# Gate tiles ahead of branch tiles in each column block, two of them before the heads' barrier, and gathered rows in a ring of eight

## The chip, the cores and the metric

The kernel runs on one core of a Trainium2 chip. The metric is device time in microseconds (us). The core has five engines that run their own instruction streams and meet by semaphores: TensorE (PE, matrix products), VectorE (DVE), ScalarE (ACT), GpSimd (POOL) and SyncE (SP, which only issues transfers here).

## The reference, cut to what matters

One decoder layer over 1024 tokens of width 1024. A wide projection feeds three branches (dilated attention, a gated recurrence, attention into memory tokens). The branches are widened, gated by sigmoids, summed and projected; then comes a layer norm, and an expert network that picks 16 of 16,384 experts for each of 8 heads of a token:

```python
branches = jnp.stack([a_out, b_out, c_out], axis=2)
gates = jax.nn.sigmoid((gate_logits + b_gate[layer]).reshape(b, s, N_BRANCHES, D_MODEL))
widened = jnp.einsum('bsgw,gwd->bsgd', branches, w_branch[layer])
merged = jnp.sum(gates * widened, axis=2)
mix = jnp.einsum('bsd,de->bse', merged, w_out[layer])
...
act = jax.nn.gelu(jnp.einsum('td,ted->te', xt, u_tab[it]), approximate=False)
return jnp.einsum('te,ted->td', gt * act, v_tab[it])
```

The gate logits are columns of the same wide projection. The dots of a token with its 128 picked rows of `u_tab` are the "gathered rows" below.

## The kernel before, in words

The layer runs in two halves of 512 tokens. Each half has these stages, parted by barriers (`cross`: TensorE, VectorE and ScalarE each drain, raise `stage`, and wait until all three have): the heads (four heads, 14 projection tiles each and the attention and recurrence work), the gated stage, the output projection, the layer norm with its transposes, and the expert queries. After both halves comes a long last stage that builds the experts' table and multiplies it, some 2300 us.

**The gated stage** runs over 8 column blocks `j` of 128 output columns. Each has six weight tiles: for each branch b a gate tile G*b* (`w_in`, 8 contraction steps, so 24 matmuls) and a branch tile B*b* (`w_branch`, 4 steps, 12 matmuls). The order is G0 B0 G1 B1 G2 B2. G*b* goes to bank `ps[0]`, ScalarE turns it into `sgate` (L1589); B*b* goes to `ps[1]`, VectorE multiplies it with `sgate` into `macc` (L2111) and adds (L2114). After three, VectorE splits the sum into `m_hi` and `m_lo`.

**A weight tile's way.** Every product is made of three: high weights times high and low data (L958, L961), then low weights times high data (L967). There are two sets of weight buffers, 0 and 1, which tiles use in turn. For each tile SyncE loads the raw weights (L651) once the buffer's last tile has been split; ScalarE copies them rounded to `w_hi` (L1383) once TensorE has begun the tile before (`w_used`); GpSimd subtracts to give `w_lo` (L848), which also frees the raw buffer. TensorE begins a tile when its `w_hi` is there, and its last third when `w_lo` is.

**Before the gated stage's branch tiles** VectorE splits the three branches' outputs into `o_hi` and `o_lo` (L2093, L2095, six instructions, `o_split` counts them), which it does after the barrier that follows the heads. B*b* waits for its two.

**Gathered rows.** In the second half the 128 rows of `u_tab` for token block 0 are gathered beside the last stages: GpSimd copies four indices (`icole`, L867) and issues an indirect transfer of 512 KB for each row (L870) into `e_ring`, 4 slots; VectorE takes the dot with `h1_up` (L1881), which frees the slot. Eight rows go with each column block, eight with each pair of output tiles, eight with each four query tiles. GpSimd issues them between its `w_lo` instructions, in the order in which the code names them (`u_rows`), and VectorE takes them in that order too (`e_rows`). The block's `h1e`, `pidxe` and `pgatee` are loaded by SyncE after the heads' barrier (`load_e_block`).

Nothing reorders instructions: on each engine they run as written.

## Time and profile before

| | |
|---|---|
| median of 3 runs | 4224.91 us (4221.99 to 4230.96) |
| the profiled execution's own time | 4228.72 us |
| its span | 4226.6 us |
| TensorE busy | 3707.9 us (88%) |
| VectorE busy | 2705.7 us (64%) |
| GpSimd busy | 1550.9 us (37%) |
| ScalarE busy | 1368.2 us (32%) |
| gated stage, first half | 556.9 to 768.8 us of the span |
| gated stage, second half | 1465.2 to 1689.4 us |

The engines overlap, so busy times do not add up to the span. What a stage could gain is read from the idle times of the engine that the others wait for in it, and from what ended them. Times in the rows are us from the span's start. "issue" means that the engine waited for nothing that the profile shows.

### The profile page before, as it was taken

The numbers are of one execution on the slowest core, as the hardware profiler recorded it, in microseconds if no ns is written. First come the engines' busy times: TensorE is split into PE (matmuls) and PEld (weight loads), VectorE is DVE, ScalarE is ACT, GpSimd is POOL, SyncE is SP. The second block draws the span as 40 slices with busy tenths as digits, with TensorE's granted clock in tenths as the row PEclk, the third lists the DMA queues.
The fourth block names the chain that finished last, engine by engine and source line by source line (L and its number), as shares of the span: only waits on it lengthen the run. The fifth ranks groups of instructions, "written<-read, shape, count | busy, mean of one in ns | idle before, by whom it ended". The sixth has DMA issues, their size and how long they took to land.

```text
span 4226.6 us, 46191 instructions
## 1 busy us (share of the span) xinstructions
PE 3707.9 (88%) x14431; PEld 2459.3 (58%) x14431; DVE 2705.7 (64%) x5477; ACT 1368.2 (32%) x2741; POOL 1550.9 (37%) x1317
## 2 busy tenths in 40 slices
PE   7999989899888799687437989799799999999998
PEld 5777867678777677475113445354354545545763
DVE  1444443307776765649899988988886878842550
ACT  1444443223434433126024042141240513314540
POOL 2555534230000176465455344443454444420000
PEclk8999999899999999796869999899899999999999
DMA  7667623355444377688999999999999999973557
GB/s 242 199 203 228 206 70 90 96 184 161 142 137 141 91 239 240 233 299 303 374 337 408 384 375 376 350 404 368 352 400 403 404 403 405 396 302 127 182 197 275
DMA packets 505249, 1133.37 MB, mean 268 GB/s; under 512 B 37932, under 2 KB 250076, under 8 KB 504832
## 3 DMA queue, kind: packets, MB, share of 16 engines
q1 hardware_dynamic: 336512, 570.42, 39.2%
q0 software_dynamic: 147456, 536.94, 33.3%
q10 hardware_dynamic: 21120, 24.12, 1.6%
q8 instruction: 70, 1.15, 0.1%
q14 instruction: 91, 0.75, 0.1%
HBM read 1044.28 MB, written 89.41 MB: 268 GB/s over the span
## 4 chain that ended last, share of the span: by engine, by line
PE 34%; DVE 13%; DMA 5%; issue 3%; ACT 1%; POOL 0%; DVEq 0%; ACTq 0%
PE ps L1277 26%; DVE u_ring L2212 6%; PE ps L1263 4%; DMA u_ring<-in_peer_u,pidx 4%; PE ps L1310 3%; DMA v_ring<-in_peer_v 1%; DVE hot L2204 1%; DVE hot L2205 1%; DVE split_v L2259 1%; ACT split_v L1688 0%; DVE pick_own L1843 0%; DVE pick_own L1848 0%; DVE got_own L1851 0%; PE h_up L1252 0%; DVE inds_own L1794 0%
## 5 line engine op out<-in xcount | busy, mean ns | idle before, releaser
L1277 PE MATMUL ps<-v_ring,table 128*128 128x512 f32 x3584 | 1595.0, 596 | 22.4 <-DMA v_ring<-in_peer_v 21.2
L899 POOL DMA_INDIRECT u_ring<-in_peer_u,pidx x896 | 861.5, 961 | 1005.1 <-DVE coefe L2212 921.2
L2212 DVE CUSTOM_DVE_ANT_0 u_ring<-u_ring,h_up 128x1024 f32<-128x1024 f32 x896 | 1061.3, 1217 | 157.2 <-DMA u_ring<-in_peer_u,pidx 145.7
L1277 PEld LDWEIGHTS ps<-v_ring,table 128*128 128x128 f32 x3584 | 664.4, 191 | 779.3 <-issue 727.3
L848 POOL TENSOR_TENSOR w_lo<-w_raw,w_hi 128x1024 fp32r<-128x1024 f32 x200 | 442.1, 2216 | 881.3 <-ACT w_hi L1383 875.7
L958 PE MATMUL ps<-x_hi,w_hi 128*128 128x512 f32 x1280 | 525.4, 410 | 68.7 <-ACT w_hi L1383 59.6
L961 PE MATMUL ps<-x_lo,w_hi 128*128 128x512 f32 x1280 | 511.8, 400 | 0.0
L1263 PEld LDWEIGHTS ps<-hot,hot 128*128 128x128 f32 x2048 | 281.1, 203 | 186.3 <-issue 104.9
L1656 ACT ACTIVATE table<-ps 128x512 f32<-128x512 f32 (+3 forms) x256 | 228.9, 894 | 426.4 <-PE ps L1263 370.4
L1644 ACT ACTIVATE hot<-hot,by_slot 128x128 f32<-128x128 f32 x1024 | 321.3, 387 | 111.3 <-DVE hot L2204 99.6
L1263 PE MATMUL ps<-hot,hot 128*128 128x128 f32 x2048 | 293.3, 289 | 61.4 <-DVE hot L2205 38.3
L958 PEld LDWEIGHTS ps<-x_hi,w_hi 128*128 128x128 f32 x1280 | 249.4, 195 | 136.8 <-ACT w_hi L1383 43.6
L967 PE MATMUL ps<-x_hi,w_lo 128*128 128x512 f32 x1280 | 316.3, 389 | 0.0
L2204 DVE TENSOR_TENSOR hot<-keys,by_slot 128x512 f32<-128x512 f32 x256 | 177.0, 692 | 178.5 <-PE ps L1263 155.9
L961 PEld LDWEIGHTS ps<-x_lo,w_hi 128*128 128x128 f32 x1280 | 249.1, 195 | 53.0 <-issue 1.9
L967 PEld LDWEIGHTS ps<-x_hi,w_lo 128*128 128x128 f32 x1280 | 240.3, 188 | 50.0
L1881 DVE CUSTOM_DVE_ANT_0 e_ring<-e_ring,h_up 128x1024 f32<-128x1024 f32 x128 | 155.3, 1221 | 167.1 <-DMA e_ring<-in_peer_u,icole 149.7
L856 POOL TENSOR_TENSOR w_hi<-w_raw,zero 128x1024 fp32r<-128x1024 f32 x56 | 111.5, 1991 | 260.9 <-PE ps L958 122.3
L1310 PE MATMUL ps<-split_v,split_c 128*128 128x512 f32 x768 | 186.3, 398 | 2.5 <-DVE split_v L2259 1.0
L1383 ACT ACTIVATE w_hi<-w_raw 128x1024 fp32r<-128x1024 f32 (+1 forms) x144 | 131.9, 916 | 145.6 <-DMA w_raw<-in_w_branch 41.5
L2205 DVE TENSOR_TENSOR hot<-keys,by_slot 128x512 f32<-128x512 f32 x256 | 175.6, 686 | 0.0
L1310 PEld LDWEIGHTS ps<-split_v,split_c 128*128 128x128 f32 x768 | 139.6, 188 | 49.0 <-DVE split_v L2259 19.5
(294 smaller groups left out, 4077.5 us busy)
## 6 DMA issues: line engine op xcount, KB each, us to landing
v_ring<-in_peer_v SPq DMA_DIRECT2D x576, 512.0 KB
w_raw<-in_w_in SPq DMA_DIRECT2D x104, 512.0 KB
wh_d<-w_hi SPq DMA_DIRECT2D x56, 512.0 KB, 2.7
wl_d<-w_lo SPq DMA_DIRECT2D x56, 512.0 KB, 4.2
w_hi<-wh_d SPq DMA_DIRECT2D x56, 512.0 KB, 3.7
w_lo<-wl_d SPq DMA_DIRECT2D x56, 512.0 KB, 3.7
w_raw<-in_w_peer_q SPq DMA_DIRECT2D x32, 512.0 KB
u_ring<-in_peer_u,pidx POOLq DMA_INDIRECT x896
```

The lines of the kernel that those rows point to most:

```text
L848: pool.tensor_tensor(out=w_lo[b][:, 0:k, :], in0=w_raw[b][:, 0:k, :], in1=w_hi[b][:, 0:k, :].bitcast(F32), op=ALU.subtract).then_inc(w_spl ...
L899: pool.indirect_dma_start(out=u_ring[:, slot_of(n, k), :], out_offset=None, in_=u_tab, in_offset=bass.IndirectOffsetOnAxis(ap=pidx[n % 2][ ...
L958: first = pe.matmul(out, w_hi[b][:, k, :], hi[:, k, :], start=(k == 0), stop=False)
L961: pe.matmul(out, w_hi[b][:, k, :], lo[:, k, :], start=False, stop=False)
L967: last = pe.matmul(out, w_lo[b][:, k, :], hi[:, k, :], start=False, stop=(k == k_n - 1))
L1263: last = pe.matmul(build_bank(item)[:, P * m:P * m + P], hot2[sub % 2][:, m, :], hot1[sub % 2][:, m, :], start=True, stop=True)
L1277: last = pe.matmul(ps[2 * (n % 2) + c][:, :], table[:, row_of(n, i1), :], v_ring[:, j % V_TILES, HALF * c:HALF * c + HALF], start=(n == p ...
L1310: last = pe.matmul(ps[2 * (n % 2) + c][:, :], c_of[:, n % 2, a, :], v[:, HALF * c:HALF * c + HALF], start=(n == p and i == 0 and a == 0 an ...
L1644: last = act.activation(hot1[sub % 2][:, m, :], hot1[sub % 2][:, m, :], ACT.Copy, scale=by_slot[:, 2, t0 + m:t0 + m + 1])
L1656: last = act.activation(table[:, r0:r0 + near, t0:t0 + TOK].rearrange("p i t -> p t i"), src[:, :, 0:near], ACT.Copy)
L2204: dve.tensor_tensor(out=hot1[sub % 2][:, :, :], in0=numbers(NTILE * (n % 2)), in1=of(0), op=ALU.is_equal).then_inc(hot_one, 1)
L2212: dve.tensor_tensor_reduce(out=u_ring[:, slot_of(n, k), :], in0=u_ring[:, slot_of(n, k), :], in1=h1_up[:, :, :].rearrange("p c n -> p (c n)"),
```

## The change

Four things are changed, in both halves where not said otherwise.

1. In a column block the three gate tiles come first, then the three branch tiles: G0 G1 G2 B0 B1 B2. Each has a bank of its own (`ps[0]` to `ps[5]`). With two sets of buffers in turn, G0, G2 and B1 use set 0, and G1, B0 and B2 use set 1.
2. TensorE's G0 and G1 of column block 0 stand ahead of the barrier that follows the heads, and so do ScalarE's three high parts for G0, G1 and G2. Column block 0 stands outside ScalarE's loop.
3. In the second half the raw weights of G0 and G1 are loaded before the heads instead of after them. G2's are loaded ahead of the wait for the barrier, the rest behind it and behind `load_e_block`.
4. The gathered rows have eight slots: `e_ring` and four more (`e_more`), which lie over memory that the branches and the heads use. GpSimd waits once for each four rows (not for each row), and besides for `o_split` 12, which is when all of the second half's branch splits are done. In the gated stage two rows each go behind the `w_lo` of G2, B0, B1 and B2, none behind G0's and G1's. Before, one or two went behind each of the six.

The diff, cut to its core:

```diff
 E_ROWS = 4
+E_SLOTS = 2 * E_ROWS
...
+MID_K = [D // P] * 3 + [4] * 3
...
+        e_more = [nc.alloc_sbuf_tensor_at(f"e_more{i}", [P, D], F32, offset=o)
+                  for i, o in enumerate((where["causal"], where["state"], where["state"] + 4 * D, where["bmv"] + 64))]
...
-        MP = Steps(sem("mid_pe"), "G0 B0 G1 B1 G2 B2".split())
+        MP = Steps(sem("mid_pe"), "G0 G1 G2 B0 B1 B2".split())
...
+        def e_row(s):
+            return e_ring[:, s, :] if s < E_ROWS else e_more[s - E_ROWS][:, :]
...
-                b, m = t // 2, T_MID // 2 + NT_MID // 2 * j + t // 2
-                if t % 2 == 0:
+                b, m = t % 3, T_MID // 2 + NT_MID // 2 * j + t // 2
+                if t < 3:
...
                 load_topk()
+                for t in range(2):
+                    mid_weight(LATER, 0, t)
                 with sp.Fori(0, NH) as h:
...
-                for t in range(2):
-                    mid_weight(LATER, 0, t)
+                mid_weight(LATER, 0, 2)
                 sp.wait_ge(tk_out, 32 * NB + 32)
                 sp.wait_ge(stage, 3 * boundary(1, 1))
                 load_e_block()
-                for t in range(2, NT_MID):
+                for t in range(3, NT_MID):
...
-            def u_rows(first, last, group, slot):
+            def u_rows(first, last, turn):
+                slot = E_SLOTS * turn
                 for k in range(first, last):
-                    s, r, g = k % E_ROWS, k // E_ROWS % 2, group + k // E_ROWS
-                    pool.wait_ge(e_dots, E_ROWS * g + s + 1)
+                    s, r, g = k % E_ROWS, k // E_ROWS, 2 * turn + k // E_ROWS
                     if s == 0:
+                        pool.wait_ge(e_dots, E_ROWS * g + E_ROWS)
                         pool.wait_ge(e_blk, 48)
+                        pool.wait_ge(o_split, 12)
...
                     for t in range(NT_MID):
-                        split_lo_only(t % 2, t0 + T_MID // 2 + NT_MID // 2 * j + t // 2, KD if t % 2 == 0 else NH)
-                        if hf == 1:
-                            u_rows(E_MID * t // NT_MID, E_MID * (t + 1) // NT_MID, E_MID // E_ROWS * j, E_MID * j)
+                        split_lo_only(t % 2, t0 + T_MID // 2 + NT_MID // 2 * j + t // 2, MID_K[t])
+                        if hf == 1 and t >= 2:
+                            u_rows(E_SLOTS * (t - 2) // 4, E_SLOTS * (t - 1) // 4, j)
...
+                def gated(j, t):
+                    it = KD * hf + j
+                    b = t % 3
+                    n = (t % 2, t0 + T_MID // 2 + NT_MID // 2 * j + t // 2)
+                    if t < 3:
+                        pe.wait_ge(MA.sem, MA.after(f"s{b}", it - 1))
+                        last = tile(n, x_hi, x_lo, KD, ps[b][:, :])
+                    else:
+                        pe.wait_ge(MV.sem, MV.after(f"g{b}", it - 1))
+                        pe.wait_ge(o_split, 6 * hf + 2 * b + 2)
+                        last = tile(n, o_hi[:, NH * b:NH * b + NH, :], o_lo[:, NH * b:NH * b + NH, :], NH, ps[3 + b][:, :])
+                    last.then_inc(*MP.mark(f"{'GB'[t // 3]}{b}"))
+                pe.wait_ge(V.sem, V.after("vt2", NH * hf + NH - 1))
+                gated(0, 0)
+                pe.wait_ge(AC.sem, AC.after("q2", NH * hf + NH - 1))
+                gated(0, 1)
                 cross(pe, boundary(hf, 1))
...
-                for t in range(NT_MID):
+                for t in range(2, NT_MID):
                     gated(0, t)
-                    if hf == 1 and t == 0:
+                    if hf == 1 and t == 2:
                         pe.wait_ge(e_blk, 48)
...
-                cross(act, boundary(hf, 1))
-                with act.Fori(0, KD) as j:
+                def mid_hi(j, t):
+                    weight_hi(t % 2, t0 + T_MID // 2 + NT_MID // 2 * j + t // 2, MID_K[t])
+                def mid_gates(j):
                     it = KD * hf + j
                     for b in range(3):
-                        n = t0 + T_MID // 2 + NT_MID // 2 * j + b
-                        weight_hi(0, n)
-                        weight_hi(1, n, NH)
                         act.wait_ge(MP.sem, MP.after(f"G{b}", it))
                         act.wait_ge(MV.sem, MV.after(f"g{b}", it - 1))
-                        act.activation(sgate[:, b, :], ps[0][:, :], ACT.Sigmoid,
+                        act.activation(sgate[:, b, :], ps[b][:, :], ACT.Sigmoid,
                                        bias=cols[:, bass.ds(KD * b + j, 1)]).then_inc(*MA.mark(f"s{b}"))
+                        mid_hi(j, 3 + b)
+                for t in range(3):
+                    mid_hi(0, t)
+                cross(act, boundary(hf, 1))
+                mid_gates(0)
+                with act.Fori(1, KD) as j:
+                    for t in range(3):
+                        mid_hi(j, t)
+                    mid_gates(j)
...
-            dve.sem_inc(e_dots, E_ROWS)
+            dve.sem_inc(e_dots, E_SLOTS)
...
-                            e_rows(2 * b, 2 * b + 2, E_MID // E_ROWS * j, E_MID * j)
+                            e_rows(2 * b, 2 * b + 2, j)
...
-                        dve.tensor_tensor(out=macc[:, min(b, 1), :], in0=ps[1][:, :], in1=sgate[:, b, :], op=ALU.mult).then_inc(*MV.mark(f"g{b}"))
+                        dve.tensor_tensor(out=macc[:, min(b, 1), :], in0=ps[3 + b][:, :], in1=sgate[:, b, :], op=ALU.mult).then_inc(*MV.mark(f"g{b}"))
```

Where the instructions stand. First ScalarE at the end of the first half's heads. L1581 and L1405 are the ends and heads of loops, `stage` is the barrier's semaphore. Before:

```order
L1581 UNCONDITIONAL_BRANCH [waits spilled2,spilled1,spilled0,stage]
L1581 ISA
L1380 REGISTER_ALU [waits w_landed0]
L1383 ACT_TABLE_LOAD [waits w_used0]
L1383 ACTIVATE w_hi0_62<-w_raw0_60 128x1024 [waits w_saved0]
L1383 ACTIVATE w_hi1_63<-w_raw1_61 128x512 [waits w_landed1,w_used1,w_saved1]
L1587 ISA
L1588 ISA [waits mid_pe]
L1589 ISA [waits mid_dve]
L1589 ACT_TABLE_LOAD
L1589 ACTIVATE sgate_122<-ps0,cols_54 128x512
```

The same place in the changed kernel, where L1397 is the high part and L1602 the gate:

```order
L1397 ACTIVATE w_hi0_62<-w_raw0_60 128x1024 [waits w_landed0,w_used0,spilled2,spilled0,spilled1,w_saved0]
L1397 ACTIVATE w_hi1_63<-w_raw1_61 128x1024 [waits w_landed1,w_used1,w_saved1]
L1397 ACTIVATE w_hi0_62<-w_raw0_60 128x1024 [waits w_landed0,w_used0,w_saved0]
L1602 ACT_TABLE_LOAD [waits mid_dve,mid_pe]
L1602 ACTIVATE sgate_122<-ps0,cols_54 128x512 [waits stage]
L1397 ACTIVATE w_hi1_63<-w_raw1_61 128x512 [waits w_landed1,w_used1,w_saved1]
L1602 ACTIVATE sgate_122<-ps1,cols_54 128x512 [waits mid_dve,mid_pe]
L1397 ACTIVATE w_hi0_62<-w_raw0_60 128x512 [waits w_landed0,w_used0,w_saved0]
```

The wait for `stage` has moved behind three high parts, and the first high part no longer has a table load ahead of it. In the row of the gate the wait for `mid_pe` (G0 done on TensorE) now comes ahead of the load of the table.

Then ScalarE's loop over the later column blocks. Before, it is the second part of the fence above (L1383 and L1589, each with a table load). In the changed kernel:

```order
L1394 REGISTER_ALU [waits w_landed0]
L1397 ACTIVATE w_hi0_62<-w_raw0_60 128x1024 [waits w_used0,w_saved0]
L1397 ACTIVATE w_hi1_63<-w_raw1_61 128x1024 [waits w_landed1,w_used1,w_saved1]
L1393 ISA
L1394 REGISTER_ALU [waits w_landed0]
L1397 ACTIVATE w_hi0_62<-w_raw0_60 128x1024 [waits w_used0,w_saved0]
L1600 ISA
L1601 ISA [waits mid_pe]
L1602 ISA [waits mid_dve]
L1602 ACTIVATE sgate_122<-ps0,cols_54 128x512
L1397 ACTIVATE w_hi1_63<-w_raw1_61 128x512 [waits w_landed1,w_used1,w_saved1]
```

No table load is left inside the loop: the block ahead of the loop leaves the sigmoid's table in place, and the copies run with it.

Last, GpSimd in the second half's gated stage, from the first `w_lo` that has a gather behind it. Before, this is G0's:

```order
L848 TENSOR_TENSOR w_lo_64<-w_raw_60,w_hi_62 128x1024 [waits w_split0]
L864 ISA
L867 ISA [waits e_blk,e_dots]
L867 COPY icole<-pidxe 128x4
L868 REGISTER_ALU
L870 DMA e_ring<-in_peer_u,icole 128x1024 [waits e_idx]
L848 TENSOR_TENSOR w_lo_65<-w_raw_61,w_hi_63 128x512 [waits w_split1]
L864 REGISTER_ALU
L870 DMA e_ring<-in_peer_u,icole 128x1024 [waits e_dots]
L847 ISA
L848 TENSOR_TENSOR w_lo_64<-w_raw_60,w_hi_62 128x1024 [waits w_split0]
```

In the changed kernel it is G2's (the third of the block), and L856 is `w_lo`, L877 the index copy, L880 the gather:

```order
L856 TENSOR_TENSOR w_lo_64<-w_raw_60,w_hi_62 128x1024 [waits w_split0]
L874 ISA
L877 ISA [waits o_split,e_blk,e_dots]
L877 COPY icole<-pidxe 128x4
L878 REGISTER_ALU
L880 DMA e_ring<-in_peer_u,icole 128x1024 [waits e_idx]
L880 DMA e_ring<-in_peer_u,icole 128x1024
L856 TENSOR_TENSOR w_lo_65<-w_raw_61,w_hi_63 128x512 [waits w_split1]
L880 DMA e_ring<-in_peer_u,icole 128x1024 x2
L855 ISA
L856 TENSOR_TENSOR w_lo_64<-w_raw_60,w_hi_62 128x512 [waits w_split0]
```

The index copy now waits for `o_split` besides, and B0's `w_lo` (128x512, buffer 65) stands behind it and behind two gathers.

## Rows read from the trace of the kernel before

**Rows 1.** Windows view, TensorE's idle span, both gated stages: us, busy us by engine, clock

```profile
544.60:556.90 12.30, 0.01 (x1) 0.01 (x1) 9.28 (x9) 10.01 (x9) 0.05 (x1) 0.61 0.00 0
556.90:768.80 211.90, 202.58 (x864) 162.29 (x864) 72.49 (x58) 74.25 (x86) 95.77 (x48) 0.99 0.31 91
585.30:768.80 183.50, 175.63 (x756) 140.82 (x756) 57.90 (x49) 64.66 (x75) 82.73 (x42) 1.00 0.32 92
1465.20:1689.40 224.20, 208.57 (x868) 166.12 (x868) 136.97 (x195) 74.21 (x86) 162.18 (x128) 0.97 0.71 232
1494.30:1689.40 195.10, 180.09 (x756) 144.00 (x756) 115.11 (x176) 64.61 (x75) 137.78 (x112) 0.97 0.71 235
1523.00:1527.00 4.00, 4.00 (x12) 3.09 (x12) 3.07 (x7) 0.63 (x1) 3.19 (x3) 0.57 0.06 16
```

**Rows 2.** Timeline of TensorE, first half: start, us, instruction, [idle before, releaser]

```profile
556.92 0.77 PE L958 MATMUL ps<-x_hi,w_hi 128*128 128x512 f32 x1 [12.31 <-ACT w_hi L1383]
...
585.32 0.50 PE L958 MATMUL ps<-x_hi,w_hi 128*128 128x512 f32 x1 [0.91 <-ACT w_hi L1383]
...
594.22 0.50 PE L958 MATMUL ps<-x_hi,w_hi 128*128 128x512 f32 x1 [0.45 <-ACT w_hi L1383]
```

**Rows 3.** Timeline of ScalarE, around the first barrier and in the loop

```profile
551.94 0.63 ACT L1418 ACTIVATE msum<-msum 128x512 f32<-128x512 f32 x1
554.42 1.28 ACT L1383 ACT_TABLE_LOAD   x1 [1.85 <-DVEq L574]
555.72 1.06 ACT L1383 ACTIVATE w_hi<-w_raw 128x1024 fp32r<-128x1024 f32 x1
...
582.91 1.28 ACT L1383 ACT_TABLE_LOAD   x1 [0.32 <-DMA w_raw<-in_w_in]
...
591.24 1.28 ACT L1589 ACT_TABLE_LOAD   x1 [4.68 <-PE ps L967]
...
593.12 1.05 ACT L1383 ACTIVATE w_hi<-w_raw 128x1024 fp32r<-128x1024 f32 x1
...
1520.35 1.28 ACT L1383 ACT_TABLE_LOAD   x1 [2.31 <-DMA w_raw<-in_w_in]
```

**Rows 4.** Timeline of SyncE's queue, two raw-weight loads

```profile
578.30 0.37 SPq L651 DMA_DIRECT2D w_raw<-in_w_in  x1
...
1513.90 0.37 SPq L651 DMA_DIRECT2D w_raw<-in_w_in  x1
```

**Rows 5.** Timeline of VectorE, the branch split, and a gathered row

```profile
554.15 1.23 DVE L2093 CAST o_hi<-branch 128x2048 fp32r<-128x2048 f32 x1
555.41 2.29 DVE L2095 TENSOR_TENSOR o_lo<-branch,o_hi 128x2048 fp32r<-128x2048 f32 x1
557.62 3.40 DVE L2093 CAST o_hi<-branch 128x2048 fp32r<-128x2048 f32 x1
...
1519.04 1.22 DVE L1881 CUSTOM_DVE_ANT_0 e_ring<-e_ring,h_up 128x1024 f32<-128x1024 f32 x1 [0.91 <-DMA e_ring<-in_peer_u,icole]
```

**Rows 6.** Timeline of GpSimd, second half's gated stage

```profile
1472.96 1.27 POOL L848 TENSOR_TENSOR w_lo<-w_raw,w_hi 128x512 fp32r<-128x512 f32 x1
...
1509.25 0.18 POOL L867 COPY icole<-pidxe 128x4 uint32 x1
1510.24 0.98 POOL L870 DMA_INDIRECT e_ring<-in_peer_u,icole  x1 [0.81 <-POOL icole L867]
1511.24 2.42 POOL L848 TENSOR_TENSOR w_lo<-w_raw,w_hi 128x1024 fp32r<-128x1024 f32 x1
1513.82 0.95 POOL L870 DMA_INDIRECT e_ring<-in_peer_u,icole  x1 [0.16 <-issue]
```

**Rows 7.** Timeline of TensorE, second half

```profile
1522.76 0.50 PE L958 MATMUL ps<-x_hi,w_hi 128*128 128x512 f32 x1 [2.90 <-ACT w_hi L1383]
...
1697.09 0.79 PE L958 MATMUL ps<-m_hi,w_hi 128*128 128x512 f32 x1 [7.89 <-ACT w_hi L1383]
```

**Rows 8.** Waits of GpSimd, second half's output projection: us, times, longest

```profile
POOL icole L867 <- DVE dotse L1881: 3.8, 2, 3.0
```

More of the change, by code:

```diff
@@ L73 @@
 E_ROWS = 4
+E_SLOTS = 2 * E_ROWS
 E_GROUPS = SLOTS // E_ROWS
[L75 to L77 removed]
+OUT_TURN = D // P
+PQ_TURN = OUT_TURN + D // P // 2
 C_Q, C_K, C_V = 0, G * NH * P, 2 * G * NH * P
@@ L385, in layer @@
         coef = coefe
+        assert where["bmv"] + 64 + 4 * D <= r_head and where["state"] + 8 * D <= where["w_raw0"]
+        e_more = [nc.alloc_sbuf_tensor_at(f"e_more{i}", [P, D], F32, offset=o)
+                  for i, o in enumerate((where["causal"], where["state"], where["state"] + 4 * D, where["bmv"] + 64))]
         split_v = [[nc.alloc_sbuf_tensor_at(f"split_v{part}_{i}", [P, D], F32R, offset=where["u_ring"] + (2 * i + part) * D * 4)
@@ L476, in layer @@
         e_blk = sem("e_blk")
-        e_in = [sem(f"e_in{s}") for s in range(E_ROWS)]
+        e_in = [sem(f"e_in{s}") for s in range(E_SLOTS)]
         e_idx, e_moved = sem("e_idx"), sem("e_moved")
@@ L1871, in topk_gates, with e_rows @@
                                   in1=tk.gsm[:, 1, :].unsqueeze(2).to_broadcast([P, PH, TOPK]), op=ALU.mult).then_inc(*TK.mark("gate"))
-            def e_rows(first, last, group, slot):
+            def e_rows(first, last, turn):
+                slot = E_SLOTS * turn
                 for k in range(first, last):
-                    s, r, g = k % E_ROWS, k // E_ROWS % 2, group + k // E_ROWS
+                    s, r, g = k % E_ROWS, k // E_ROWS, 2 * turn + k // E_ROWS
                     if s == 0:
@@ L1879, in e_rows @@
                         dve.wait_ge(e_moved, g + 1)
[L1880 to L1881 removed]
+                    dve.wait_ge(e_in[k % E_SLOTS], 16 * turn + 16)
+                    dve.tensor_tensor_reduce(out=e_row(k % E_SLOTS), in0=e_row(k % E_SLOTS), in1=h1_up[:, :, :].rearrange("p c n -> p (c n)"), scale=1.0, scalar=0.0,
                                              op0=ALU.mult, op1=ALU.add, accum_out=dotse[:, r, s:s + 1]).then_inc(e_dots, 1)
                     if s == E_ROWS - 1:
[L1884 removed]
+                        dve.wait_ge(e_dots, E_ROWS * g + E_ROWS + E_SLOTS)
                         dve.tensor_copy(coefe[:, bass.ds(slot + k - s, E_ROWS)], dotse[:, r, :]).then_inc(e_moved, 1)
```

31 lines of the change are left out of this document (9 added, 22 removed).

## The prediction

> **What bounds the kernel now.** I read the windows view over the stages first, then TensorE's timeline for its idle times and their releasers, then the timelines of the engines that those name. TensorE is what the others wait for in the gated stages. In a column block of the first half it stands twice for ScalarE's high part: 0.45 us at G1 and 0.6 to 0.9 us at the next G0 [rows 2]; blocks 1 to 7 take 183.5 us, 26.2 each. In the second half the same seven take 195.1 us, 27.9 each [rows 1]: there the raw weights are late. All three gate tiles used buffer set 0, so that each began with a chain of w_lo 2.4, raw load, high part 1.06. A load without gathers beside it takes from 578.30 to 582.9, 4.6 us [rows 3, 4]; with them, from 1513.90 to 1520.35, 6.45 us [rows 3, 4], and TensorE then stood 2.9 us and fell to the lower clock [rows 1, 7].
>
> **Part 1: two tiles ahead of the barrier.** It sounds as if 10.9 us of work went into the 12.3 us gap. It does not, for the high part of G0 still stands on ScalarE behind the last head's tail, which ends at 551.94 + 0.63 = 552.6 [rows 3]. What goes is the wait for the barrier, 1.85 us, and a table load, 1.28 us: the high part starts near 552.8, ends near 553.9, and TensorE starts near 554.1, 2.8 us earlier than at 556.92 [rows 2, 3]. G0 keeps its half clock. G0 and G1 then end near 567. But TensorE is now the last at the barrier, and VectorE's split of the branches, which began at 554.15, begins near 567.4. Its six instructions take 3 x (1.23 + 2.29) = 10.6 us if nothing disturbs them; beside GpSimd's w_lo the same copy took 3.40 us [rows 5]. I take 11.8, so the third split is there at 579.2. G2 ends at 573.1, B0 at 575.8, B1 at 578.5, B2 waits 0.7 and ends near 582.2, and the next G0 follows: 3.1 us ahead of 585.32 [rows 2]. Bounds: 0 (the split at 13.9 as disturbed by two w_lo of 5.3 us, and a drain of about 1 us) to 4.
>
> **Part 2: gates first, own banks, no table loads in the loop.** Each loop turn now lacks two loads of 1.28 us [rows 3]. At G1 the chain of load, gate and high part made the 0.45 us and goes whole. At the next G0 what is late next is the raw load: it is issued when B1's w_lo is done. From the block's start: B0 starts at 16.4, high part of B1 until 17.6, w_lo (1.27, [rows 6]) until 19.0, raw load (4.6 with issue) until 23.6, high part until 24.8, so TensorE starts near 24.9 instead of 24.6, and a stop costs 0.25 more, since the first matmul takes 0.50 instead of 0.39 and the pipe refills [rows 2]. A block takes 25.2 us instead of 26.2: 7.0 us over seven. Bounds: 0.4 a block (load 0.9 us slower) to 1.6 (no stop), so 3 to 11.
>
> The Trainium skill (ScalarE: Activation LUTs, "What ACT_TABLE_LOAD costs") puts a switch at 1283 ns and a drain of some 1380 ns more. The load agrees [rows 3]; here the high part starts 0.02 us behind its load, without a drain. By the page the two loads would have cost 5.3 us a turn and part 2 would bring up to 11 us.
>
> **Part 3: the second half's block 0.** Start near 1462.4, again 2.8 us early, G1's end near 1475.5, barrier, G2 until 1481.3, h1_up until 1482.6, B0's high products until 1484.5. The e block and B0's raw weights are issued behind the barrier and are there by 1482, about in time. The price lies on GpSimd: it waits for `o_split` 12 behind G2's w_lo, and B0's w_lo is queued behind that wait and two gathers. The split ends at 1475.8 + 10.8 = 1486.6. Then index copy and its wait 1.0, two gathers 2.3, w_lo 1.3 [rows 6]: near 1491.4. TensorE stands 7 us there, which brings the lower clock again for 4 us (2 us lost). B2's w_lo and the next G0's raw load are late too, by 2 us and 1 us. I lay the next G0 at 1502.5 against 1494.3 before [rows 1]: 8 us lost. Bounds: 4 to 12. Nothing hides it; VectorE's dots only come later.
>
> **Part 4: blocks 1 to 7 of the second half.** GpSimd's work is the same, three w_lo of 2.42, three of 1.3, two index copies of 1.0 and eight gathers of 1.25 [rows 6], 23.2 us with gaps, but it is laid anew: none of it behind G0 and G1, where it waits for raw weights, all of it behind the rest. Its round is w_lo G0 2.4, raw load of G2 4.6, high part 1.2, w_lo G2 2.4, copy and two gathers 3.3, w_lo B0 1.3, two gathers 2.4, w_lo B1 1.3, copy and two 3.3, w_lo B2 1.3, two 2.4: 25.9 us, above TensorE's 24.6. With gathers beside the loads a load takes up to 1.85 us more and there are two on the round (G2's and the next G0's). I take 26.5 between 25.9 and 29.6, nearer the low end because the gathers in flight are fewest when G2's load runs. Against 27.9 that gives 1.4 x 7 = 9.8 us. Bounds: -12 to +14. The eight slots take away GpSimd's waits for dots, which in this stage were none above the gaps of issue.
>
> **Part 5: the edges behind.** At the stage's end VectorE takes the last two dots, then m_hi and m_lo, then comes the barrier; TensorE idled 7.9 us [rows 7]. The last gather now starts about 0.4 us behind B2's end; landing 5.2 [rows 5, 6], dot 1.3, copy and splits 1.6, barrier to product 1.3: 9.8 us, so 1.9 lost (bounds 0 to 4). In the output projection GpSimd stood 3.8 us in two waits for dots [rows 8]; the ring takes them, but behind the longer one its w_lo would have waited for a high part that was itself late by its raw load. I take 1.5 (0 to 3.8). The query tiles: 0.5 (0 to 2.5). Loading two raw tiles before the second half's heads brings nothing: their high parts did not wait for them.
>
> **The sum**, in the profiled execution's own time: 3.1 + 7.0 - 8.0 + 9.8 - 1.9 + 1.5 + 0.5 = 11.9, some 12 us gained (the 2.8 us of the second half's early start are in its 8.0). The last stage does not change and moves as a whole. Its 4228.7 lies 3.8 us above the median of 4224.9, inside the runs' spread, so I subtract from the median, and since the load under gathers is more likely longer than I took than shorter, I take off 1 us: 4224.9 - 11 = 4214.
>
> **The rivals.**
> - *A (slower): the bunched gathers stretch the raw loads.* In blocks 1 to 7 of the second half both loads on GpSimd's round take the 6.45 us of [rows 3, 4]: 29.6 us a block, 1.7 x 7 = 12 us lost where 9.8 was won. With block 0 at its bound of 12 lost and the edges 3 lost: 3.1 + 7 - 12 - 12 - 3 + 1 = -16, so 4241. It decides from a block of about 28.9 us on, or a load of 6.1 us. For it: eight gathers now fall in 60% of the block. Against: G2's load runs while no gather is issued. Chance 0.12.
> - *B: second half breaks even or worse, the first half carries it all.* Block 0 loses 8, the blocks win 4 to 6, edges lose 1: total near 6, 4219, no change by measurement. Chance 0.28.
> - *C: the ring and the order free GpSimd fully.* Block at 25 us in both halves, block 0 loses 5: 3.1 + 8 - 5 + 18 + 1 = 25, so 4200. Against: the 25.9 us round. Chance 0.12.
> - *D: the tiles ahead of the barrier fill the whole gap.* It would need ScalarE's high part before its tail ends; the order shows it behind. 9 us more in each half; chance 0.02.
> - My forecast: 0.46.
>
> **How the numbers follow.** A measurement here tells about 0.2%, 8.4 us, from no change. Faster is C, D, 0.39 of the forecast's 0.46 (its terms spread by about 5 us) and 0.03 of B: 0.56. Slower is A less its mild cases: 0.10. The same is the rest, 0.34. The range reaches to C's outer half and to A's inner third: 4201 to 4228.
>
> **What would show it.** In the profile after: TensorE's first product of each gated stage 2 to 3 us earlier, not 10; no table loads in the loop, stops at G1 gone; a single wait of TensorE for GpSimd's w_lo of about 7 us in the second half's block 0, with the index copy behind the last `o_lo`; first half's seven blocks at 25.2 us, second half's at 26.5 us; the idle at the stage's end near 9.8 us. I am wrong if the second half's blocks take over 28 us, if the splits don't hold GpSimd, or if B2 of block 0 waits over 3 us in the first half.

## The result, and the profile after

| | before | after |
|---|---|---|
| median | 4224.91 us | 4237.87 us (4233.01 to 4239.97) |
| ratio of the times | 1 | 1.0028, 95% interval 1.0017 to 1.0040 |
| span of the profiled execution | 4226.6 us | 4236.0 us |

The change made the kernel 0.28% slower, some 12 us. The forecast was 11 us faster, 4214, with a range of 4201 to 4228. It was wrong in sign, and the time lies outside the range.

The windows view of the changed kernel, to be laid beside [rows 1]: the idle ahead of the first gated stage, that stage up to its last product, its block 0, its blocks 1 to 7, and in the second half the whole stage, its blocks 1 to 7, and 4 us behind the stop in block 0. The columns are those of [rows 1].

```profile
546.80:555.80 9.00, 0.01 (x1) 0.00 (x0) 6.18 (x7) 8.61 (x8) 0.01 (x1) 0.65 0.00 0
555.90:758.60 202.70, 200.02 (x864) 164.34 (x864) 69.56 (x59) 54.81 (x72) 93.16 (x48) 0.98 0.32 93
555.80:587.00 31.20, 28.47 (x108) 22.71 (x109) 17.39 (x10) 8.20 (x10) 17.11 (x7) 0.88 0.27 77
587.00:758.60 171.60, 171.58 (x757) 141.70 (x755) 52.27 (x50) 46.61 (x62) 76.15 (x41) 1.00 0.33 96
1457.30:1689.20 231.90, 210.18 (x868) 165.33 (x868) 123.84 (x193) 54.76 (x72) 155.15 (x128) 0.97 0.68 220
1496.60:1689.20 192.60, 178.74 (x756) 141.47 (x756) 106.03 (x174) 46.56 (x62) 135.57 (x112) 0.99 0.73 235
1485.70:1489.70 4.00, 3.91 (x9) 3.13 (x10) 2.10 (x3) 0.00 (x0) 3.33 (x5) 0.50 0.92 307
```

The first half does what was hoped and more: 202.7 us instead of 211.9, and in blocks 1 to 7 TensorE is busy for 171.58 of 171.6 us. The second half's stage went from 224.2 to 231.9 us, though its blocks 1 to 7 gained 2.5. So what was lost is in its block 0. Some more was lost outside the two gated stages. TensorE's timeline of the changed kernel, only the rows that began after a wait:

```profile
582.65 0.47 PE L968 MATMUL ps<-o_hi,w_hi 128*128 128x512 f32 x1 [2.40 <-issue]
...
939.38 2.07 PE L1014 MATMUL h_up<-skt_side,qs_side 128*128 128x128 f32 x8 [4.81 <-DMA qs_side<-qp_d]
...
1485.79 2.07 PE L977 MATMUL ps<-o_hi,w_lo 128*128 128x512 f32 x4 [6.13 <-POOL w_lo L856]
...
1496.62 0.50 PE L968 MATMUL ps<-x_hi,w_hi 128*128 128x512 f32 x1 [1.48 <-ACT w_hi L1397]
...
1560.72 0.47 PE L968 MATMUL ps<-x_hi,w_hi 128*128 128x512 f32 x1 [1.80 <-ACT w_hi L1397]
...
1700.50 0.80 PE L968 MATMUL ps<-m_hi,w_hi 128*128 128x512 f32 x1 [11.32 <-ACT w_hi L1397]
...
1723.78 0.79 PE L968 MATMUL ps<-m_hi,w_hi 128*128 128x512 f32 x1 [7.83 <-ACT w_hi L1397]
```

The same places in the kernel before:

```profile
945.88 1.38 PE L1004 MATMUL h_up<-skt_side,qs_side 128*128 128x128 f32 x8 [1.99 <-DVEq L574]
...
1715.54 0.80 PE L958 MATMUL ps<-m_hi,w_hi 128*128 128x512 f32 x1 [4.00 <-issue]
```

Read them as five places. At 939 the first score product of the second half waits for its queries, where it waited 2.0 us for the barrier before. At 1485.79 is the stop that the forecast described. At 1560.72 TensorE stops at G1 of a later block; the next G0s have stops too, as at 1496.62. At 1700.50 the idle behind the gated stage has grown from 7.9 [rows 7] to 11.3 us. At 1723.78 a stop in the output projection has doubled.

By stages, each number the difference of the starts of two such rows in one trace (the two traces of each kernel; the heads and the last stage scatter):

| stage | before, twice | after, twice |
|---|---|---|
| first gated stage to first product of the projection | 216.2, 216.4 | 207.1, 206.4 |
| that to first scores of the second half | 172.8, 173.3 | 176.4, 177.1 |
| scores to second G0 (heads) | 519.3, 517.1 | 517.9, 513.0 |
| second G0 to first product of the projection | 231.9, 228.4 | 243.2, 242.7 |
| output projection to query tiles | 97.7, 97.8 | 99.7, 98.5 |
| query tiles to key_f | 104.6, 106.5 | 103.0, 104.7 |
| last stage | 2327.2, 2329.1 | 2332.7, 2332.0 |

Without the heads and the last stage, which the change does not touch, these stages take 823.2 and 822.4 us before, 829.5 and 829.4 us after: some 7 us lost by the traces.

### The profile page after: what moved, and what is told of

The parts are those of the page before. It is cut to its first block, busy times and chain, and to the rows that moved or that the text cites. A ratio compares the mean times of both kernels' runs of the same rounds, so it can differ in the third digit from the quotient of the medians.

```text
span 4236.0 us, 46052 instructions
## 1 busy us (share of the span) xinstructions
PE 3717.9 (88%) x14431; PEld 2468.9 (58%) x14431; DVE 2689.4 (63%) x5477; ACT 1326.3 (31%) x2711; POOL 1542.2 (36%) x1317
## 3 DMA queue, kind: packets, MB, share of 16 engines
q1 hardware_dynamic: 336512, 570.42, 39.3%
## 4 chain that ended last, share of the span: by engine, by line
PE 33%; DVE 14%; DMA 5%; issue 2%; ACT 1%; POOL 0%; DVEq 0%; ACTq 0%
PE ps L1291 26%; DVE u_ring L2236 6%; DMA u_ring<-in_peer_u,pidx 4%; PE ps L1277 4%; PE ps L1324 2%; DVE split_v L2283 1%; ACT split_v L1711 1%; DMA v_ring<-in_peer_v 1%; DVE hot L2228 1%; DVE hot L2229 1%; PE h_up L1266 0%; DVE pick_own L1866 0%; DVE pick_own L1871 0%; DVE got_own L1874 0%; ACT split_c L1710 0%
## 5 line engine op out<-in xcount | busy, mean ns | idle before, releaser
L856 POOL TENSOR_TENSOR w_lo<-w_raw,w_hi 128x1024 fp32r<-128x1024 f32 (+1 forms) x200 | 443.3, 2218 | 880.2 <-ACT w_hi L1397 874.2
L1397 ACT ACTIVATE w_hi<-w_raw 128x1024 fp32r<-128x1024 f32 (+1 forms) x144 | 132.1, 917 | 396.2 <-PE ps L968 144.6
```

The lines of the kernel that those rows point to most:

```text
L856: pool.tensor_tensor(out=w_lo[b][:, 0:k, :], in0=w_raw[b][:, 0:k, :], in1=w_hi[b][:, 0:k, :].bitcast(F32), op=ALU.subtract).then_inc(w_spl ...
```

## The experiments

Each ratio is against the kernel before, run in turn with it on the same chip. The last column is the sum of the stages above without the heads and the last stage, in the run's trace; the kernel before has 823.2 and 822.4.

| run | ratio | 95% interval | stages, us |
|---|---|---|---|
| the change itself | 1.0028 | 1.0017 to 1.0040 | 829.5, 829.4 |
| x1_raw_back | 1.0002 | 0.9992 to 1.0013 | 834.5 |
| x2_group | 1.0004 | 0.9994 to 1.0014 | 828.9 |
| x3_spread | 0.9975 | 0.9966 to 0.9984 | 821.6 |
| x4_projdots | 1.0010 | 1.0001 to 1.0019 | 829.1 |
| y1_shift | 0.9980 | 0.9968 to 0.9991 | 818.5 |
| y2_ring_alone | 1.0000 | 0.9988 to 1.0011 | 824.0 |
| y3_ring4 | 1.0009 | 1.0000 to 1.0019 | 823.6 |
| y4_small | 0.9969 | 0.9960 to 0.9979 | 815.6 |
| z3_half | 0.9965 | 0.9952 to 0.9978 | 810.4 |
| z4_barrier_back | 0.9997 | 0.9985 to 1.0009 | 820.0 |
| w1_first_half | 0.9971 | 0.9960 to 0.9983 | 818.8 |

The variants ran in four series on four chips, and none of these holds the changed kernel beside them, but for one execution: 4229.68 us, beside 17 of the kernel before with a median of 4227.67. So what a variant gains over the changed kernel by the difference of two ratios is uncertain by some 7 us. In all eleven runs that difference is also larger than what the traces show, by 2 to 16 us. So 1.0028 may lie somewhat above the change's usual cost: the spans of the two pairs of traces differ by 9.4 and 3.3 us. Where times and traces disagree below, the size of a part is taken from the trace.

**x1_raw_back.**

```diff
-                for t in range(2):
-                    mid_weight(LATER, 0, t)
                 with sp.Fori(0, NH) as h:
...
-                mid_weight(LATER, 0, 2)
+                for t in range(3):
+                    mid_weight(LATER, 0, t)
```

> The changed kernel, with the raw weights of the second half's G0 and G1 loaded behind the heads again, as before the change. Theory (a small load behind big ones): in the changed kernel TensorE waited 4.8 us for the first queries at the start of the second half's heads, because two raw loads of 512 KB stood ahead of theirs on SyncE's queue, and only 2.0 us before the change; that wait goes back to about 2, the heads end 4 to 5 us sooner, and G0's high part still finds its weights. About 4233 against 4238. Rival (the wait is the query load's own, whatever stands ahead): no difference, 4238, the 4.8 us stay.

Measured: 1.0002 instead of 1.0028. The wait is gone, and G0's high part was not late (TensorE's idle ahead of it is 9.05 and 9.06 us). TensorE's first scores in this run:

```profile
932.47 1.15 PE L1013 MATMUL h_up<-skt_side,qs_side 128*128 128x128 f32 x8 [2.15 <-DVEq L581]
```

SyncE's queue in the changed kernel and, behind it, before:

```profile
930.67 1.00 SPq L658 DMA_DIRECT2D w_raw<-in_w_in  x2
932.09 2.73 SPq L687 DMA_DIRECT2D qs_side<-qp_d  x1
```

```profile
939.62 0.39 SPq L680 DMA_DIRECT2D qs_side<-qp_d  x1
```

The issue of the queries' load alone took 2.73 us instead of 0.39, behind 1 MB of raw weights which nobody needed for 500 us. In the eight traces with the raw loads ahead of it this issue took 2.06 to 3.56 us, in the other seven 0.39. TensorE stood 2.8 us longer and ran at the lower clock behind it (granted 0.55 from 940 to 946). The trace shows 3 us for the wait and its clock; the time moved by more (0.26%, 11 us, with an uncertainty of about 7). The first theory stands, with 3 us by the trace; the 11 us are not shown. The same code in the later stages was slower in this trace (195.2 us for blocks 1 to 7), so that its sum of stages can't settle the size.

**x2_group.**

```diff
-                        pool.wait_ge(o_split, 12)
+                        if r == 1:
+                            pool.wait_ge(o_split, 12)
```

> The changed kernel, but GpSimd waits for o_split 12 only before the second four of each eight gathers (the new slots, which lie over the branches' memory), not before the first four. Theory (the queue behind the wait): B0's w_lo is no longer behind the splits, the stop of 6.1 us in the second half's block 0 goes; the next wait is at B2, whose w_lo now stands behind the o_split wait and two gathers: 1.5 to 3 us. Gain 3 to 5 us, 4233 to 4235 against 4238. Rival (the splits set it): GpSimd's w_lo and index copy now run beside VectorE's splits, which take 13 us instead of 10.5, so TensorE waits for o_split instead and gains 0 to 1 us: 4237.

Measured: 1.0004. Block 0 took 37.0 us instead of 39.3, so 2.3 of the 6 to 8 us that the stop cost. VectorE's splits were not slower (10.5 us in both), which refutes the rival. It was GpSimd that was, once the e block had landed and its index copy could go at 1473.11. Its timeline:

```profile
1474.25 2.45 POOL L881 DMA_INDIRECT e_ring<-in_peer_u,icole  x1 [0.96 <-POOL icole L878]
1477.01 2.71 POOL L881 DMA_INDIRECT e_ring<-in_peer_u,icole  x1 [0.30 <-issue]
1479.74 1.27 POOL L856 TENSOR_TENSOR w_lo<-w_raw,w_hi 128x512 fp32r<-128x512 f32 x1
```

A gather's instruction took 2.45 and 2.71 us beside the splits, where it takes 0.95 elsewhere [rows 6]. So B0's w_lo still came 3.2 us late. Neither theory had that, though the trace of the kernel before has it too, with 2.59 and 2.83 us. In the six traces where gathers run beside VectorE's splits, all twelve of them took 2.45 to 2.83 us; none of the 1966 others took over 1.46.

**x3_spread.**

```diff
+                for t in range(NT_MID):
+                    split_lo_only(...)
+                    if hf == 1 and t >= 2:
+                        u_rows(E_SLOTS * (t - 2) // 4, E_SLOTS * (t - 1) // 4, 0)
-                with pool.Fori(0, KD) as j:
+                with pool.Fori(1, KD) as j:
...
-                        if hf == 1 and t >= 2:
-                            u_rows(E_SLOTS * (t - 2) // 4, E_SLOTS * (t - 1) // 4, j)
+                        if hf == 1:
+                            u_rows(E_SLOTS * t // NT_MID, E_SLOTS * (t + 1) // NT_MID, j)
```

> The changed kernel, with the gathers of column blocks 1 to 7 of the second half laid behind all six w_lo (1, 1, 2, 1, 1, 2), as before the change, instead of 0, 0, 2, 2, 2, 2. Theory (bunching makes G1's raw load late): in the changed kernel these blocks took 27.5 us, with stops of 0.2 to 1.9 us at G1 because B2's w_lo ends late and G1's raw weights are loaded behind it. Spread, the stop at G1 goes and a new one may come at G2: 26.5 us a block, 7 us less, 4231. Rival (the number of gathers counts, not their place): GpSimd's round is the same, and the gathers now run beside G0's and G1's raw loads as well, 27.5 to 28 a block: 4238 to 4241.

Measured: 0.9975, as the theory had it. Its blocks 1 to 7 in the windows view:

```profile
1493.50:1679.80 186.30, 177.36 (x756) 144.91 (x756) 111.15 (x176) 46.62 (x62) 136.27 (x113) 0.97 0.77 249
```

That is 26.6 us a block against 27.5. The number of gathers and GpSimd's busy time are the same (136 us), only their place differs. It also leaves less idle behind the stage, 8.9 us instead of 11.3.

**y4_small.** The gathers of this stage have 64 bytes a row; the rest of each row is left out, and the dots read these bytes again and again.

```diff
-                    pool.indirect_dma_start(out=e_row(k % E_SLOTS), out_offset=None, in_=u_tab,
+                    pool.indirect_dma_start(out=e_row(k % E_SLOTS)[:, 0:w], out_offset=None, in_=u_tab if w == D else u_small,
```

> The changed kernel, with the gathers of the second half's gated stage fetching 16 elements of a row (64 bytes) instead of 1024; the dots read these 16 again and again, over 1008 elements. So part of the gathered data is left out, while GpSimd's and VectorE's instructions stay. Theory (contention): the raw loads come back to 4.6 us, GpSimd's round is 25.9 us, and blocks 1 to 7 take 25.9 to 26.3 instead of 27.5: 9 to 11 us less, 4228. Rival (GpSimd's own time is the bound, not the memory): the blocks stay at 27 or more: 4235 to 4238.

Measured: 0.9969, more than expected. Its blocks 1 to 7:

```profile
1495.60:1674.30 178.70, 175.71 (x757) 140.57 (x756) 109.52 (x175) 46.68 (x63) 134.69 (x113) 1.00 0.34 95
```

25.5 us a block, with the same busy time of GpSimd. This separates the two: 2.0 us a block, 14 us in all (12 against the second trace), is what the gathers' traffic costs through the raw loads. G1's raw weights show it best, whose load starts as the gathers behind B1 and B2 are in flight. The issue on SyncE's queue (the first of a row that holds two) and the high part that waits for it, changed kernel:

```profile
1551.38 5.20 SPq L658 DMA_DIRECT2D w_raw<-in_w_in  x2
```

```profile
1559.52 1.06 ACT L1397 ACTIVATE w_hi<-w_raw 128x1024 fp32r<-128x1024 f32 x1 [6.39 <-DMA w_raw<-in_w_in]
```

With small gathers:

```profile
1547.05 5.23 SPq L659 DMA_DIRECT2D w_raw<-in_w_in  x2
```

```profile
1550.93 1.06 ACT L1398 ACTIVATE w_hi<-w_raw 128x1024 fp32r<-128x1024 f32 x1 [3.25 <-DMA w_raw<-in_w_in]
```

8.1 us from issue to high part against 3.9. Over the seven blocks of the changed kernel the load of G1 took 6.6 to 8.3 us, that of the next G0 5.1 to 5.9, that of G2 5.0 to 6.3. The kernel before had 6.45 at worst where I looked [rows 3, 4]; four gathers close together give more than that.

**x4_projdots.** In the output projection `u_rows` is called with a flag:

```diff
+                    if each:
+                        pool.wait_ge(e_dots, E_ROWS * g + s + 1 + E_ROWS)
```

> The changed kernel, but in the output projection each gather waits until the dot four before it is done, as with the ring of four. Theory (gathers that run on stretch the loads): in the changed kernel the raw weights of the third tile landed 19.7 us after they were issued, 14.8 us before the change, as eight gathers ran without a break beside them and the load of the residual; TensorE's stop there was 7.8 us against 4.0. With the waits back it is 4 to 5 us and the projection 3 us shorter: 4235. Rival (the load is late for its own reasons, mainly the 2 MB of the residual): the stop stays 7.8 and the waits cost up to 2 us: 4238 to 4240.

Measured: 1.0010, projection 98.1 us (99.7 and 98.5 in the changed kernel), and the stop fell from 7.8 to 3.4:

```profile
1719.10 0.50 PE L970 MATMUL ps<-m_hi,w_hi 128*128 128x512 f32 x1 [3.43 <-ACT w_hi L1399]
```

The raw load behind the stop took 15.2 us from issue to high part, 19.7 in the changed kernel. Waits of GpSimd for dots, which held nothing up themselves, had kept the gathers away from a late load. In all eight traces with the ring of eight and without these waits the stop is 6.8 to 9.5 us, in the five with a ring of four or with these waits and the gathers in their old turns 3.4 to 4.2.

**y2_ring_alone.** The kernel before with `E_SLOTS`, `e_row` and `e_more`, the wait per four rows, and `o_split` 12 ahead of the new slots.

> The kernel before with one part of the change alone: eight slots for the gathered rows, one wait for dots per four rows (and for o_split 12 before the first use of the new slots). Order of tiles, barrier and loads as before. Theory (the ring is worth nothing or a little less): GpSimd had no waits for dots in the gated stage, and in the output projection the 3.8 us of waits go but the raw load there is stretched by gathers that run on: 4229, the same as before within 3 us, with TensorE's stop in the projection going from 4.0 to about 7. Rival (the prediction's own: the ring gains in the projection): 1.5 to 3.8 us faster, stop at or below 4.0.

Measured: 1.0000, and the stop in the projection is there without any other part of the change. The raw weights had been issued at 1698.76 and the high part started at 1717.62:

```profile
1718.73 0.79 PE L967 MATMUL ps<-m_hi,w_hi 128*128 128x512 f32 x1 [7.48 <-ACT w_hi L1392]
```

The rival, which was the forecast's term of +1.5, falls by the trace: the projection took 98.9 us, not less than the 97.7 before. The time alone could not tell 1.5 us.

**y3_ring4.** The changed kernel with `e_ring` alone and its old waits.

> The changed kernel with all of it but the ring: four slots, each gather waits for the dot four before it, no wait for o_split. Theory (the ring's wait for o_split costs more than its slots bring): block 0's stop of 6.1 us falls to about 3, as in the run without that wait for the first four, the projection's stop falls from 7.8 to 4 or 5, and in blocks 1 to 7 GpSimd waits a little for dots, 0 to 0.5 us a block: 3 to 6 us faster than the changed kernel, 4233. Rival (with two gathers behind each of four tiles the ring of four is too short): GpSimd stands over 1 us a block for dots, G1's raw weights come later still: 4245 or more.

Measured: 1.0009, 0.19% less than with the ring of eight (uncertain by 0.15%). The stop in the projection is 3.7 us. GpSimd's waits for dots over the whole stage (us, times, longest):

```profile
POOL e_ring L879 <- DVE dotse L1904: 4.2, 6, 0.8
```

Four slots are nearly enough even where the gathers are bunched. The ring brought nothing in any run, and its wait for the splits cost 2.5 us in block 0 (36.8 against 39.3).

**z4_barrier_back.** In the second half alone:

```diff
+                if hf == 1:
+                    cross(pe, boundary(hf, 1))
                 pe.wait_ge(V.sem, V.after("vt2", NH * hf + NH - 1))
                 gated(0, 0)
...
-                for t in range(3):
+                for t in range(3 - 2 * hf):
                     mid_hi(0, t)
                 cross(act, boundary(hf, 1))
+                if hf == 1:
+                    mid_hi(0, 1)
+                    mid_hi(0, 2)
```

> The changed kernel, but in the second half TensorE's G0 and G1 stand behind the barrier again, and so do ScalarE's high parts of G1 and G2. Theory (TensorE as the last at the barrier sets when the branch splits begin): the splits begin at the heads' end instead of 13 us later, GpSimd's wait for o_split 12 ends before B0 is needed, the stop of 6.1 us in block 0 goes, at the price of 1 to 2 us of barrier ahead of G0: next G0 5 to 7 us earlier, 4232. Rival (the stop has another cause, as B0's raw weights or the e block, which are loaded behind the barrier as well): the stop stays above 3 us, 4236 to 4239.

Measured: 0.9997. The stop of 6.1 us is gone (stops of 0.6 and 1.4 us for w_lo remain), G0 waits 9.51 us instead of 9.06, and block 0 takes 32.9 us instead of 39.3. G0's high part still stands ahead of the barrier here. So the two tiles themselves gain 0.45 us ahead of G0, and cost 6.4 us behind it, once a split and GpSimd's queue hang on that barrier; the rest of the earlier start is the high part's.

**y1_shift.** `x1_raw_back` and `x4_projdots`, and the gathers a turn later:

```diff
+                        if hf == 1:
+                            u_rows([0, 2, 4, 6, 7, 8, 8][t], [0, 2, 4, 6, 7, 8, 8][t + 1], j - 1)
+                if hf == 1:
+                    u_rows(0, E_SLOTS, KD - 1)
```

> A version meant to mend what the runs so far found: the changed kernel with the raw weights of the second half's G0 and G1 behind the heads again, the waits for single dots back in the output projection, and the gathers moved: none in column block 0, in blocks 1 to 7 those of the block before (2, 2, 2, 1, 1, 0 behind the six w_lo), the last eight after the stage's last w_lo, where GpSimd idled 10.6 us; their dots stand behind the barrier. Theory (each loss is one of order): block 0 from 39.3 to about 32 us, blocks 1 to 7 from 27.5 to 26.3, idle at the edge from 11.3 to about 8, start of the heads 4 less, output projection no gain since w_lo of its second tile waits for the dots: 7 + 8 + 3 + 4 = 22 us less than the changed kernel, 4216, bounds 4206 to 4222. Rival (memory traffic is what it is; a stop removed comes back as another): about the x3 kernel's 4217 less the 4 of the heads, with block 0 as slow as before since the raw loads then are the bound, 4226.

Measured: 0.9980, 4220, between the theory and its rival. Block 0 fell to 28.8 us, better than expected. But the pattern 2, 2, 2, 1, 1, 0 gave blocks of 27.5 us (bunched again, now at the gate tiles), and eight dots behind the barrier made the projection's second w_lo late (projection 104.4 us):

```profile
1699.03 3.49 PE L982 MATMUL ps<-m_hi,w_lo 128*128 128x512 f32 x8 [9.66 <-POOL w_lo L855]
```

**z3_half.** The same by half a turn, and spread:

```diff
+                            at_t = (0, 1, 2, 4)
+                            if t < 3:
+                                u_rows(4 + at_t[t], 4 + at_t[t + 1], j - 1)
+                            else:
+                                u_rows(at_t[t - 3], at_t[t - 2], j)
```

> A second mended version. As the first (raw weights of G0 and G1 behind the heads; single waits for dots in the projection), but the gathers are moved by half a turn only: in block 0 two behind B1 and two behind B2, in blocks 1 to 7 1, 1, 2, 1, 1, 2 behind the six w_lo as in the spread run, the last four behind the stage's last w_lo, with their dots behind the barrier. The wait for o_split 12 stands before the new slots alone. Theory: block 0 30 to 32 us (39.3 in the changed kernel), blocks 1 to 7 26.6 (27.5), edge idle 8 to 9 (11.3), heads 4 less, projection 98 (99.7) since the first gathers there need only two dots made behind the barrier: 8 + 6 + 3 + 4 + 2 = 23 us less than the changed kernel's 4238, 4215, and below both mended parts alone. Rival (the projection takes it back as in the first mended version, where w_lo waited 9.7 us for dots): projection 103, 4221.

Measured: 0.9965, 4209, faster than both kernels. Its block 0, and its blocks 1 to 7:

```profile
1448.90:1480.30 31.40, 28.78 (x112) 22.41 (x113) 14.77 (x10) 8.20 (x10) 17.20 (x10) 0.93 0.37 107
1480.30:1666.20 185.90, 175.96 (x757) 143.39 (x755) 118.19 (x176) 46.61 (x62) 139.54 (x114) 0.98 0.77 250
```

31.4 and 26.6 as expected, the edge 6.3 us; only the projection took 103.0 us instead of 98, as its rival had warned. By the time (five executions) it is not told apart from w1_first_half, which leaves the second half as it was; by the stages' sums it is 8 us faster than that.

**z1_before_again and z2_after_again.** No edit, one trace each.

> The kernel before, unchanged, for one more trace. In the ten traces so far the last stage (from the transposes of key_f to the end, the same instructions in all) took 2327.2 and 2327.0 us in the two kernels with the former order of the gated stage and 2328.7 to 2337.1 us in the eight with the new one. Theory (it scatters by itself, by some 3 us): anything from 2325 to 2334. Rival (something of the new order carries into it): 2327 within 1.

> The changed kernel, unchanged, for one more trace. Theory (the last stage scatters by itself): anything from 2327 to 2336 us there, while the stages before it repeat within 1 us each: G0 to next G0 39.3, blocks and edge 203.9, projection 99.7, first wait for queries 4.8. Rival (the last stage is lengthened): 2332.7 within 1.

Their stages are in the table above. What belongs to the change repeats within 1.2 us; the blocks 1 to 7 of the kernel before took 195.1 us in one trace and 190.8 in the other, those of the changed kernel 192.6 and 191.1. So the 2.5 us gained there are no more than scatter: over all traces these blocks took 190.8 to 195.6 us in the four with the former order, and 190.8 to 195.2 in the seven with the new order and its bunched gathers. The last stage is looked at below.

**w1_first_half.** The kernel before with the new order in the first half only; `MP2` is the old list of steps for the second.

```diff
+                new = skip == 0
-                b, m = t // 2, T_MID // 2 + NT_MID // 2 * j + t // 2
+                b, m = t % 3 if new else t // 2, T_MID // 2 + NT_MID // 2 * j + t // 2
...
-                        dve.wait_ge(MP.sem, MP.after(f"B{b}", it))
+                        dve.wait_ge(MP.sem, (MP2 if hf else MP).after(f"B{b}", it))
```

> The kernel before, with the change in the first half's gated stage alone (gates first, own banks, two tiles ahead of the barrier, no table loads in the loop); everything of the second half, the ring of four and the later loads of raw weights as before. Theory (the parts add, and the last stage's extra 4 us are not the order's doing or scatter): the first half gains 10 to 12 us as in the traces of the changed kernel and the rest is untouched, 4217, ratio 0.9974, last stage 2327 to 2330. Rival (the new order costs some 4 us in the last stage, wherever it stands): 4221, ratio 0.9984, last stage 2331 or more.

Measured: 0.9971, 12 us faster. The first gated stage with its edge took 207.0 us, as in the changed kernel. So the first half's part is worth 12 us by itself. The second half's part cost the difference between 1.0028 and 0.9971, 0.57% or 24 us (uncertain by some 7) by the times, and 11 us by the stages' sums.

## Why the prediction was wrong, point by point

**Part 1** (3.1 forecast). TensorE's idle fell from 12.3 to 9.05 us, 3.25 gained where I had 2.8, by the steps I gave. But block 0 took 31.2 us, 2.8 more than the 28.4 from 556.92 to 585.32 [rows 2]: the splits took 13.6 us (568.91 to 582.55 on VectorE) and not 11.8, B2 waited 2.40 us and not 0.7 (the row names no releaser, but it starts 0.1 us behind the last split), and the clock was low behind it (0.58 granted from 583 to 587, rows of 0.63 us a matmul until 585.4). VectorE's last split:

```profile
579.30 3.25 DVE L2119 TENSOR_TENSOR o_lo<-branch,o_hi 128x2048 fp32r<-128x2048 f32 x1
```

Net 0.5. I had 0 as the lower bound, with just this reason.

**Part 2** (7.0). Blocks 1 to 7 took 171.6 us instead of 183.5, 12 gained: there is no stop at all. The term that was mis-sized is the raw load ahead of the next G0. I took 4.6 us from one load [rows 3, 4]; in these blocks it takes 3.9 to 4.0 us from issue to high part. What stands before it ran as I had laid it: in block 1, which starts at 587.06, B1's w_lo was done 18.8 us in (I had 19.0). SyncE's and ScalarE's rows of the load and of the high part:

```profile
606.15 0.37 SPq L658 DMA_DIRECT2D w_raw<-in_w_in  x1
```

```profile
610.14 1.06 ACT L1397 ACTIVATE w_hi<-w_raw 128x1024 fp32r<-128x1024 f32 x1 [2.90 <-DMA w_raw<-in_w_in]
```

TensorE began that G0 at 611.54, 0.3 us behind the end of the high part, and did not wait. Why the load is 0.6 us shorter than the one in the kernel before no run shows. The 12 us are 7.9 us of idle (183.5 less 175.63 busy, [rows 1]) and 4.1 us by which TensorE's busy time fell, as no matmul follows a stop any more.

By the Trainium skill (ScalarE: Activation LUTs, "What ACT_TABLE_LOAD costs"), which adds a drain of some 1380 ns to each switch of table, this part would have brought, as an estimate, up to 11 us. That comes near the 12, but by another road: no row here has the drain (the high part of [rows 3] starts 0.02 us behind its load), and the 12 are accounted for without it.

Both parts together: 10.1 forecast, 12.4 in the trace, 12.3 in the run of this part alone.

The raw loads ahead of the heads: I said they bring nothing, since no high part waited for them. That was the right reading and half the question. I did not ask what stands behind them on SyncE's queue. It cost 3 to 4 us in the traces; the 11 us by the time are not shown.

**Part 3** (-8.0). Right. G0 to next G0 went from 29.1 to 39.3 us, less the 3.25 of the earlier start: -7.0. The stop for w_lo is 6.1 us, the index copy waited 12.4 us, until the last `o_lo` was done:

```profile
1480.94 0.18 POOL L877 COPY icole<-pidxe 128x4 uint32 x1 [12.40 <-DVE o_lo L2119]
```

The clock granted behind it was 0.50. That it comes from TensorE as the last at the barrier and from GpSimd's wait is shown by z4_barrier_back (block 0 6.4 us shorter) and, for a part, by x2_group (2.3 us).

**Part 4** (+9.8). This is the step that failed most. I took 26.5 us a block against 27.9. Measured were 27.5, and 27.3 in the second trace, where the kernel before had 27.3 too: 2.5 gained in the one pair, none in the other. The order of GpSimd's work was read right. The size of a raw load under gathers was not: I took up to 1.85 us more, on the ground that few gathers are in flight when G2's load runs. But G1's load, which I left out of the round, starts between the gathers of B1 and B2, and took 8.1 us (6.6 to 8.3 over the blocks). Without the traffic the block is 25.5 us, below my round of 25.9, so that this round was not the bound. Rival A had this mechanism. It lost less here than A's 12 us, since the two loads that A names stayed below its 6.45 us (5.1 to 5.9 and 5.0 to 6.3); the time came near A's 4241 by other roads.

**Part 5** (-1.9, and +1.5 for the projection). The idle behind the stage is 11.3 us instead of 9.8: -3.4. In the projection the ring's freed gathers delayed the raw load and the stop grew from 4.0 to 7.8: 1 to 2 us lost, where I had a gain. I had counted the waits that go, not what those waits had kept apart.

**The last stage** (0). It took 2327.0 to 2329.3 us in the four traces with the former order in the second half, and 2328.4 to 2337.1, 2331.8 on average, in the eleven with the new one. Its instructions are the same. w1_first_half lies at 2329.3, so nothing speaks for a hand of the first half in it. Whether 4 us of the change are lost here or the stage scatters is open: no run takes the two apart.

Summed over the profiled pair: +12.4 first half, -3.6 to the first scores, -7.0, +2.5, -3.4, -2.0, +1.6 query tiles, -5.5 last stage, -4 in the heads, which are unchanged and scatter: 9 us lost, as the spans show. My seven terms add up to 12.0 and not 11.9, and rival C's block of 25 us would be worth 20 us in seven blocks, not 18; neither matters here. The chances had 0.10 for slower. They leaned on one large term, 9.8 with bounds of -12 to +14, whose lower half I called less likely on an argument and not on a row.

## What to carry to other kernels

A wait that costs nothing may be what keeps two transfers apart, and a load issued early takes the queue from whatever comes next: ask of each freed or moved transfer what it runs beside. Work put ahead of a barrier makes its engine the last one there; look first at what the others have queued behind that barrier. Where other transfers run beside a load that the bound engine needs, spread them evenly: the same gathers, spread, made a block 0.9 us shorter and the idle behind the stage 2.4 us. And put a kernel and its variants into one series where a difference of a few us is to be read from times.

## What the runs showed of the hardware

- A 512 KB load took 3.9 us from issue to the copy that waits for it with 64-byte gathers beside it (y4_small), and 8.1 us with four gathers of 512 KB around it; blocks 1 to 7 took 7% less with small gathers (178.7 us for 192.6).
- GpSimd's gather instruction took 2.45 to 2.83 us in all twelve cases beside VectorE's splits, against a median of 0.95 us and at most 1.46 among the 1966 others.
- The issue of a 256 KB load behind two of 512 KB on one queue took 2.06 to 3.56 us in eight traces, against 0.39 in the seven without them.
